# Opening of an expert retrieval: order of small turns, of eight projection units and of a norm among the gathers

## The reference, cut to what matters

```
x   = x + g1x * (o @ w_out)                # o: the attention's output
hx2 = modulate(rmsnorm(x, norm2_g), sh2x, sc2x)
q = (hx2 @ w_q).reshape(C, 8, 2, 128)      # 8 heads, two halves of a key
s = einsum('chpd,hpnd->chpn', q, subkeys)  # 128 scores for each half
sv, si = top_k(s, 16)                      # then the best 16 of the 16 x 16 sums
best, pos = top_k(sv0[:, None] + sv1[None, :], 16)
ids = row numbers of the 16 experts;  g = softmax(best)
a = gelu(einsum('cd,chkd->chk', xc, u[ids]))
y = einsum('chk,chkd->cd', g * a, v[ids]);   x = x + g2x * y
```

## Time and profile before

| | us |
|---|---|
| median of three runs | 1747.97 (1747.78 to 1748.62) |
| the profiled execution | 1741.25 |
| its span, first to last instruction | 1739.5 |
| first gather to last gather issued | 227.6 to 927.0 |
| TensorE busy in the span | 1446.3 (83%) |
| VectorE busy | 895.4 (51%) |
| ScalarE busy | 561.8 (32%) |
| mean traffic of the DMA engines | 329 GB/s |

### The profile page before, as it was taken

One profiled execution on the slowest core, in us unless ns is written; L12 is line 12 of the kernel. 1 busy time (PEld: TensorE's weight loads), 2 busy tenths in 40 slices (PEclk: granted clock), 3 DMA queues, 4 the chain that ended last, 5 costly groups with the idle time before them and its releaser, 6 DMA issues.

```text
span 1739.5 us, 21127 instructions
## 1 busy us (share of the span) xinstructions
PE 1446.3 (83%) x7808; PEld 881.0 (51%) x7808; DVE 895.4 (51%) x2104; ACT 561.8 (32%) x1402; POOL 294.6 (17%) x277
## 2 busy tenths in 40 slices
PE   5999876877886767666656999999989999999997
PEld 4586743534542223333112899887744454544343
DVE  4787577476666666666765887522131212111112
ACT  3113467354544444444444146302121111111111
POOL 0100033233344444434441000000000000000000
PEclk8999988889989787788788999999999999999999
DMA  9771179899999999999995534453489999999994
GB/s 396 273 268 61 37 298 368 328 426 399 378 413 427 424 421 426 422 427 426 416 427 218 204 125 146 155 185 111 178 339 427 428 428 427 427 427 428 428 427 181
DMA packets 80002, 571.89 MB, mean 329 GB/s; under 512 B 9137, under 2 KB 9393, under 8 KB 11185
## 3 DMA queue, kind: packets, MB, share of 16 engines
q1 hardware_dynamic: 40608, 284.55, 40.2%
q0 software_dynamic: 39312, 286.28, 40.1%
HBM read 569.75 MB, written 1.05 MB: 328 GB/s over the span
## 4 chain that ended last, share of the span: by engine, by line
PE 53%; DMA 26%; DVE 13%; ACT 4%; issue 2%; POOL 1%; SPq 0%; DVEq 0%; POOLq 0%; ACTq 0%
DMA big<-in_peer_dram,misc 15%; PE bank L1689 12%; DMA big<-in_moe_down_dram 10%; PE bank L1496 8%; PE bank L1337 7%; DVE big L2000 5%; PE bank L1134 4%; PE bank L1282 2%; PE bank L1138 2%; PE bank L1677 2%; PE bank L1564 2%; DMA ring<-in_first_dram 1%; PE bank L1359 1%; POOL big L620 1%; PE bank L1248 1%
## 5 line engine op out<-in xcount | busy, mean ns | idle before, releaser
L1337 PE MATMUL bank<-big 128*64 128x512 f32 x1024 | 311.3, 740 | 184.6 <-ACT big L796 183.1
L620 POOL DMA_INDIRECT big<-in_peer_dram,misc x256 | 285.2, 1114 | 522.8 <-PE bank L1337 366.4
L1337 PEld LDWEIGHTS bank<-big 128*64 128x64 f32 x1024 | 72.6, 158 | 361.9 <-ACT big L796 248.8
L2000 DVE SCALAR_TENSOR_TENSOR big<-big 128x1024 f32<-128x1024 f32 x128 | 155.8, 1224 | 109.4 <-DMA big<-in_peer_dram,misc 108.6
L2000 DVE SCALAR_TENSOR_TENSOR big<-big,misc 128x1024 f32<-128x1024 f32 x128 | 154.5, 1222 | 84.1 <-DMA big<-in_peer_dram,misc 83.7
L1689 PE MATMUL bank<-big 128*64 128x512 f32 x640 | 140.3, 592 | 1.3 <-ACT big L1019 1.3
L790 ACT ACTIVATE misc<-misc 128x1 f32<-128x1 f32 x256 | 51.4, 201 | 273.7 <-DVE big L2000 261.2
L1689 PE MATMUL bank<-big,misc 128*64 128x512 f32 x512 | 114.9, 596 | 19.5 <-DMA big<-in_moe_down_dram 13.4
L1496 PE MATMUL bank<-H,ring 128*128 128x256 f32 x448 | 102.3, 391 | 5.9 <-DVE H L2095 3.0
L1496 PEld LDWEIGHTS bank<-H,ring 128*128 128x128 f32 x448 | 87.9, 197 | 19.8 <-issue 7.2
L1689 PEld LDWEIGHTS bank<-big 128*64 128x64 f32 x640 | 50.7, 137 | 87.4 <-issue 85.7
(11 more groups left out here) (409 smaller groups left out, 2266.3 us busy)
## 6 DMA issues: line engine op xcount, KB each, us to landing
big<-in_moe_down_dram SPq DMA_DIRECT2D x64, 1024.0 KB, 20.0
ring<-in_second_dram SPq DMA_DIRECT2D x36, 1024.0 KB
ring<-in_first_dram SPq DMA_DIRECT2D x33, 1024.0 KB
big<-in_moe_gate_dram SPq DMA_DIRECT2D x32, 1024.0 KB, 20.4
big<-in_moe_up_dram SPq DMA_DIRECT2D x32, 1024.0 KB, 19.3
ring<-in_moe_gate_dram SPq DMA_DIRECT2D x32, 1024.0 KB, 22.2
misc<-in_mod_rest_dram POOLq DMA_DIRECT2D x16, 1024.0 KB, 6.0
big<-in_moe_far_up_dram SPq DMA_DIRECT2D x16, 1024.0 KB, 23.9
```

The costliest lines, as they stand in the source:

```text
L620: pool.indirect_dma_start(out=gathered[b % GATHERS], out_offset=None, in_=t["peer"], in_offset=bass.IndirectOffsetOnAxis(ap=rows[:, b % 32 ...
L1337: last = nc.tensor.matmul(bank[2 * tt + half][HALF * g:HALF * (g + 1), :], diag[:, b % DIAGS, :], gathered[b % GATHERS][:, a:a + 512], sta ...
L2000: dve.scalar_tensor_tensor(u, u, 1.0, x_pairs[b // (BLOCKS // 2)][:, b % 2, :], ALU.mult, ALU.mult, accum_out=dots[:, b % 32:b % 32 + 1]). ...
```

## The change

Five things are moved in the opening of the loop (stages 0 to 2). Only the order changes, no instruction is added or taken out.

- On PE, `turn_rows` (q = 3) and `turn_gate` (q = 5) come ahead of the pair's query and attention step, in all stages.
- The eight output units of the second tile: three, three and two at the pairs 14, 15 and 16 become two each at the pairs 14, 15, 16 and 17. Their adds on DVE stood ahead of the dots of the blocks 30, 32 and 34. Now they stand behind the second dot of the units' own pair, that is behind the blocks 29, 31, 33 and 35.
- The norm of the attention's output is spread: squares at block 13 (were at block 19), sum at pair 9 (was at pair 11), root at block 20 (was at block 24). DVE's `normalise_od` stays at block 25.
- The second norm goes back by a step: squares at block 36 (35), sum at pair 19 (18), root at block 40 (38), `scale_h2` at block 42 (39), `shift_h2` at block 43 (41).
- The first two queries that need both tiles move from the pairs 21 and 22 to the pairs 22 and 23.

```diff
-    ((0, 3), (0, 5), (1, 3), (1, 5), (2, 5), (2, 6), (3, 0), ...
+    ((0, 3), (0, 5), (1, 3), (1, 5), (2, 6), (2, 7), (3, 0), ...
-OUT_AT = {(1, 6): range(0, 3), (1, 7): range(3, 6), (2, 0): range(6, 8)}
-ADD_OUT_AT = {(1, 14): range(0, 3), (2, 0): range(3, 6), (2, 2): range(6, 8)}
+OUT_AT = {HALF_PAIRS + 6 + i: (2 * i, 2 * i + 1) for i in range(4)}
 # ScalarE
-                if s == 1:
-                    if c == 3:
-                        square_od(1)
+                if (s, c) == (0, 13):
+                    square_od(1)
+                if (s, c) == (1, 4):
+                    root_od1()
+                if s == 2:
+                    if c == 4:
+                        square_x1_last()
                     if c == 8:
-                        root_od1()
-                if s == 2:
-                    if c == 3:
-                        square_x1_last()
-                    if c == 6:
                         root_x1(1)
-                    if c == 9:
+                    if c == 11:
                         shift_h2(1)
 # TensorE
+                if s + 1 < STAGES:
+                    if q == 3:
+                        turn_rows(s + 1)
+                    if q == 5:
+                        turn_gate(s + 1)
+                if (s, q) == (1, 1):
+                    sum_od1()
                 if p in QUERY_AT:
                     query(QUERY_AT[p])
                 if p in ATTEND_AT:
...
-                if s + 1 < STAGES:
-                    if q == 3:
-                        turn_rows(s + 1)
-                    if q == 5:
-                        turn_gate(s + 1)
-                if (s, q) == (1, 3):
-                    sum_od1()
-                for n in OUT_AT.get((s, q), ()):
+                for n in OUT_AT.get(p, ()):
                     out_last(n)
-                if (s, q) == (2, 2):
+                if (s, q) == (2, 3):
                     sum_x1_last()
 # VectorE
-                add_out(1, ADD_OUT_AT.get((s, c), ()))
-                if (s, c) == (2, 7):
+                if (s, c) == (2, 10):
                     scale_h2(1)
                 ...
                 dot(b)
+                if c % 2 == 1:
+                    add_out(1, OUT_AT.get(b // 2, ()))
```

More of the change, by code:

```diff
@@ L56 @@
 QUERY_AT = {s * HALF_PAIRS + q: AHEAD + m for m, (s, q) in enumerate(
-    ((0, 3), (0, 5), (1, 3), (1, 5), (2, 5), (2, 6), (3, 0), (3, 1), (3, 2), (3, 3), (3, 4), (3, 5), (3, 6),
+    ((0, 3), (0, 5), (1, 3), (1, 5), (2, 6), (2, 7), (3, 0), (3, 1), (3, 2), (3, 3), (3, 4), (3, 5), (3, 6),
      (4, 0), (4, 2), (4, 4), (4, 5), (4, 6), (5, 4), (5, 6)))}
```

## The result

| us | before | changed |
|---|---|---|
| median of five runs each | 1747.78 (1742.45 to 1748.62) | 1737.53 (1732.57 to 1739.50) |
| ratio of the two, 95% interval | | 0.9944 [0.9924, 0.9964] |
| the profiled execution, and its span | 1741.25, 1739.5 | 1732.57, 1730.8 |

Timed in two more series, it gave 0.9958 [0.9944, 0.9973] and 0.9967 [0.9953, 0.9980]. The three together, weighted by the inverse square of their intervals, are 0.9959 [0.9950, 0.9968], about 7.1 us. So the first timing lay on the far side of what repeats show, and the effect to be explained is some 7 us. The ratios and intervals are those on record for a series; they aren't the quotient of the two medians, from which they can differ by more than 0.1%.

A forecast was written before the change was run, and what follows sets the result against it. Retrieval was taken as bound by transfers except in parts of its opening; -5.2 us there, +0.3 and -0.3 later cancelling, took 1741.25 to 1736.0, carried over to the timed median as 1742.8 us; range 1738.5 to 1748.5.

The forecast's parts named there:

- What bounds: Transfers bind except in stretches of the opening; at 310 to 345 us, 8.1 us lost would become 2.9, giving -5.2.
- thin queues: At 310 to 345 us, 1.7 us still lost while only one to three gathers are in flight.
- The turn ahead of the query: At block 24 the turn follows pair 10 directly, so the dot starts at 309.2 instead of 311.3: -2.1 us.
- The root's wait: At block 25 DVE's 1.28 us stop for ACT's root goes; the dot begins 3.3 us earlier in all.
- Up to pair 10 I expect no movement: Sum ahead of pair 9 and root at block 20 priced zero, up to 2 us if PE's clock is low.
- Pair 12 at the high clock: PE idles about 1.8 us ahead, adds take 1.94 us instead of 3.68; pair ends 5.1 us earlier.
- Pairs 14 to 17: Two output units a pair, some 5.6 us each; about 7 us earlier at pair 14, 10 at 17, transfers not following.
- Second norm, queries, later stages at zero: Norm behind saturated transfers: zero; crowded queries at pairs 22 to 30 +0.3, cancelled by -0.3 from later turns.
- The later turns: At pairs 27 and 29 the 0.41 us turn lies in PE's wait for key scores: bounds 0 and -0.8, taken -0.3.
- The slower one: Rival: crowded queries at pairs 23 to 27 empty the transfer queue, +3.6 us, 1751.6; chance 0.09.
- That of the gain mostly lost: Rival in the opening: pair 12's clock stays low or cover is eaten, only -2.4 us, 1745.6; chance 0.26.
- The larger one: Rival: all 8.1 us of 310 to 345 and about 1 of 412 to 437 return, -9, 1739; chance 0.10.

The follow-up runs named there:

- e5_before_again: The kernel before, unchanged, run again as a kernel of its own: 1745.84 us against 1745.05, ratio 1.0006 [0.9995, 1.0016].
- e1_again: The changed kernel timed and profiled once more with no edit: 1739.08 us against 1746.28 before, ratio 0.9958 [0.9944, 0.9973].
- e6_turns_only: The kernel before with only the small turns moved ahead of query and attention: 1744.27 us against 1745.05, ratio 0.9998 [0.9982, 1.0015].
- e4_div_early: The changed kernel with DVE's division of the first norm moved from block 25 to block 24, ahead of the row numbers: 1737.17 us, ratio 0.9945 [0.9927, 0.9963].
- e10_second_norm_only: The kernel before with only the second norm and the first two-tile queries later: 1743.65 us against 1745.52, ratio 0.9994 [0.9978, 1.0009].
- e11_div_mem: The changed kernel with the first norm's division at block 24 and the memory's norm two blocks later: 1736.65 us against 1745.52 before, ratio 0.9951.
- e3_second_half: The changed kernel with turns and first norm put back; output units, second norm and queries stay moved: 1745.27 us, ratio 1.0001 [0.9984, 1.0018].

## Why the prediction was right in its mechanism and short in its size

The measured median lies below the stated range. What failed is one term, the movement up to pair 10, put at zero, and the base and width of the range; the links that the forecast added up came out as it said.

- **What bounds.** Right. Time lost at 310 to 345, by the prediction's own formula: before 8.1 and 10.0 (e5_before_again, 305 GB/s), changed 2.5, 4.1 (e1_again, 377 GB/s) and 3.4. The means differ by 5.7; forecast 5.2. Over equal blocks, dots 20 to 43, it is 6.0. Of the forecast's 2.9 us still lost, 1.7 for thin queues came without a working; 3.3 were measured.
- **The turn ahead of the query.** Forecast -2.1 at dot 24. Turns alone moved it from 9.75 to 7.20 behind dot 23, -2.5, of which 0.2 lie in pair 10's own clock. Right.
- **The root's wait.** Forecast -1.3 between dots 24 and 25, measured 6.90 to 5.53, the same in all five profiles with the norm spread and the division in its place. Right, and e6_turns_only shows that without it the turn is worth nothing. The prediction named both links but did not say that the one would swallow the other. With pair 10's clock taken out, both together are worth 3.6 us at dot 25, forecast 3.3.
- **"Up to pair 10 I expect no movement."** This is the step that failed. It asked only whether the root would come too late (it didn't: block 21's weights were out at 297.4, the adds that need them began at 301.76), and priced the sum at PE as a delay of 1 us. It didn't ask what the sum does to the idle time that it fills. PE's wait ahead of pair 10 fell from over 4 us to about 3, and transposes and adds took 4.1 us instead of 5.3 (4.9 instead of 5.6 in the changed kernel and before alone), some of them wholly at the clock of 2.4 GHz. Dots 23 to 24 so came 2.9 closer instead of 2.1. Dot 25 stands 4.9 us sooner behind dot 20 in the mean, forecast 3.3. Of the 1.6 more, 0.7 are pair 10's, 0.3 the two links', and 0.6 lie ahead of dot 23 and are spread (below).
- **Pair 12 at the high clock.** Forecast 1.94 behind a gap of 1.8. Measured 1.94, 1.94 and 2.84 in the three profiles, behind gaps of 2.0 to 2.1. Nearly right: in the first profile the granted clock was 0.66 over these adds. The Trainium skill (TensorE: Matmul & The Clock Gate, "HAM oscillation") has gaps for data put the clock back. Behind the waits of 4.2 us and more ahead of pair 12 the rows agree (3.0 to 3.7 us). The prediction took that section to leave its gap of 1.8 us open. By the rule there, gaps as short as pair 12's are harmless; the 2.84 us behind 2.12 us differ from it, and the measurement decides. For gaps of 2 to 4 us this case shows either level, for the same program too.
- **Pairs 14 to 17.** Forecast 5.6 us each. The adds of the changed kernel start at 323.91, 329.54, 335.18 and 340.81, 5.63 apart. Right, and, as forecast, the transfers don't follow to the 10 us of lead at PE: at dot 43 it is 6.1 us. The gather of block 31 stands 22.8 to 23.2 us behind that of block 23, by the forecast's own times 23.7 to 23.9, before 28.8.
- **Second norm, queries, later stages at zero.** The second half, its two parts and the repeat of before are all within 0.2% of one. Right within what can be measured. The later turns, at pairs 27 and 29, were priced at -0.3 and lie inside dots 43 to 76, where the turns alone take 100.3 us, between the 98.6 and 101.5 of before; what they give isn't shown. Dot 43 to 76 is 1.0 us shorter in the mean, a term that I had at zero; since single executions of before differ by 2.9 us there, it isn't shown.
- **The rivals.** The slower one did not occur: changed executions move 417 to 424 GB/s at 345 to 412, a little under the 426 that was to show the forecast right. Between the dots 46 and 55, its place, they move 408 to 426, never under 400. That of the gain mostly lost named the clock at pair 12, and the clock did vary, but not enough. The larger one wanted all that was lost at 310 to 345 back; of 9.1 in the mean 3.3 are still lost.

So the term sized wrong is pair 10, put at zero and measured at 0.7 to 1.2 us. It accounts for at most that much of the missing 1.9 us (7.1 against 5.2), for a lead at dot 25 isn't kept whole: e4_div_early loses 2.4 of its 4.0 us by dot 43. The rest of it, dots 43 to 76 and 20 to 23, can't be told from spread. The other 3.1 us, up to the 10.2 of the first timing, belong to that timing: between the medians two repeats gave 7.2 and 6.3. Against the later series (before 1746.28, 1745.05 and 1745.52, changed 1739.08 and 1739.20) before was 1.5 to 2.7 us high in it and the changed kernel some 1.6 low. So the base of the forecast, the three-run median 1747.97, was some 2 us high too, a term that it took over without a bound. Both repeats of the changed kernel lie inside the stated range, and only the first timing lies below it. The profiled executions help to see how: the changed kernel's was 1.8 us ahead at dot 2 already, where nothing has been moved yet. Its dots 20 to 23 took 6.60 where the repeats have 7.69 and 7.80. Before's repeat, too, was 1.6 us ahead of before's first profile at dot 2. e10_second_norm_only, in which nothing is moved before block 36, shows 6.53 as well. So this is the program's own spread. The range was too narrow for it: it had been built from costs of the change alone, and single executions of before spread from 1735.7 to 1751.2.

ScalarE's page in the Trainium skill (ScalarE: Activation LUTs, "What ACT_TABLE_LOAD costs") adds a drain to each load of 1.28 us. In the rows above the activation of line 789 that follows the load back starts at 295.73, 0.02 behind its end, and the load for the root is done while the wait is still on. In each of the fourteen profiles 58 to 61 table loads stand between two activations with less than 0.05 us of idle time on either side. No run here shows a drain.

## What to carry to other kernels

Where an engine stands behind two waits in a row, removing the first alone can be worth nothing (here turns alone 0, norm alone -3, both -8 us): look for what is late next and move both. When a small piece of matmul work is moved, ask what it does to the idle time that it leaves and that it fills, since the clock of the next pair may hang on it. And have the spread of the program's own timings in the range: single executions of before lay 15.5 us apart, twice the effect, and medians of its series 2.7.

## What the runs showed of the hardware

- The eight adds of pair 10 took 1.94, 2.5 to 2.7 or 3.4 to 3.7 us in fourteen profiles, behind waits of 2.8 to 5.0 us ahead of the pair. Three executions of one program gave 2.56, 3.68 and 3.63 there, and 2.84, 1.94 and 1.94 at pair 12: at a gap of 2 to 4 us the order of the program alone doesn't set the level.
- The table load of ScalarE is taken ahead of the wait of the instruction that needs it (290.26, with the root at 293.73). A root that waits for its operand so pays only for the load back.
- From dot 100 to the last gather the kernels differ only in whether the turns come ahead of the queries. They take 387.8 to 391.5 us in twelve profiles. The two others are e11_div_mem (393.4), which comes there with its wait moved, and e3_second_half (394.3), which has before's order there, so that nothing in the order explains it. That is left open.
